# Six modulation chunks of the next layer: one per scan instead of all six ahead of the scans

## The chip, the cores and the metric

The kernel runs on one core of one Trainium2 chip. The metric is device time in microseconds (us) of one execution of the whole program, which computes both layers. The names of the engines here are: PE is TensorE (matrix products), DVE is VectorE, ACT is ScalarE, POOL is GpSimd, SP is SyncE, which in this kernel issues the loads of weights. PEld is the loading of the stationary operand, which goes beside PE.

## The reference, cut to what matters

One step of a diffusion backbone for 128 context and 256 latent tokens, two layers (`l` is 0, 1), model width 1024. Everything is float32.

```python
def trunk_layer(x, cvec, P, l, ctx=None, rope=None):
    mod = jnp.dot(jax.nn.silu(cvec), P['mod_w'][l]) + P['mod_b'][l]        # 1024 x 6144
    sh1, sc1, gt1, sh2, sc2, gt2 = jnp.split(mod[:, None, :], 6, axis=-1)
    h = rms_norm(x, P['norm1_g'][l]) * (1 + sc1) + sh1
    z = jnp.dot(h, P['w_in'][l])
    q, k, v, su, sv, rkv, xw, xa, xg, gates = split_cols(z, IN_SIZES)
    ...                                                # attention, gated MLP in chunks
    for d in range(2):                                 # RWKV-7, forwards and backwards
        s_fin, o_d = wkv_scan(s_init[d], r_h, heads(w_d), k_d, v_h, kk, heads(a_d), reverse=(d == 1))
    ...                                                # merge by gates, w_out
    x = x + gt1 * jnp.dot(merged, P['w_out'][l])
    h2 = rms_norm(x, P['norm2_g'][l]) * (1 + sc2) + sh2
    x = x + gt2 * moe(h2, P, l)                        # 64 experts, top 6, and a shared one

def wkv_scan(s0, r, w, k, v, kk, a, reverse):
    def step(s, inp):
        r_t, w_t, k_t, v_t, kk_t, a_t = inp
        sa = jnp.einsum('bhij,bhj->bhi', s, -kk_t)
        s = s * w_t[:, :, None, :] + sa[..., None] * (kk_t * a_t)[:, :, None, :] + v_t[..., None] * k_t[:, :, None, :]
        return s, jnp.einsum('bhij,bhj->bhi', s, r_t)
```

## The kernel before, in words

A loop runs twice, once per layer. Every engine has its program written out in order, and engines wait for each other on named semaphores; nothing is reordered by a scheduler. A layer goes through these stages: input projection (10 weight chunks), attention, gated MLP, six scans, merge, output projection, router and experts.

**Modulation.** The 6144 columns of `mod` are made in 16 chunks of 384 columns. A chunk is 1.5 MB of weights in one of two slots of SBUF (`slot0`, `slot1`). ACT copies the result to `mod_row` (`mod_rows`, line 635), and PE turns it to columns with three products with `sel` (`mod_turn`, six matmuls in the profile). Chunks 6 to 15 belong to this layer and are made during attention (10 calls, `c` from 0 to 9). Chunks 0 to 5 of the **next** layer (`c` from 10 to 15; MOD_B is 10 and MOD_A is 6) are made in one block on PE, lines 1647 to 1651, just ahead of the scans. They are gathered in PSUM bank 5 and DVE copies them to `next_mod` at once (line 1156).

**Slots.** Chunk n lies in slot n % 2. SP loads the next chunk of a slot when `slot_taken` of that slot has been raised. In the kernel before, a modulation chunk raises it with the first product of its turn, that is after ACT's copy.

**The scans.** `SCANS` lists six pairs of direction and chunk of 128 tokens, run in this order (scan 0 to 5). A scan of 128 steps is done by blocks: products of keys and queries within blocks (`block_grams`), then a triangular inverse by six levels. For each level PE does `level_y` for two groups, ACT copies the result to `YS` (line 765), PE does `level_x`, and DVE subtracts it (`invert`, line 1134); POOL prepares the block matrices `BL` (line 543). Between these, PE does `pair_grams` 0 to 3, which DVE masks (`mask_grams`, lines 1116 and 1118), and work of the scan before (`solve`, `results`) and for the scan after (`decay_or_rate`). In the last scan PE also does `bonus_and_gate` 0 to 3, and DVE the eight products of line 1191.

**What the first scan needs.** `block_grams(0)` waits for `queries_ready`, raised at line 1067 on DVE, the end of the chain of lines 1148 (a reciprocal of 128x1540 elements), 1149, 1058, 1062, 1066 and 1067. Lines 1071 to 1081 come behind it and raise `keys_ready`.

**PSUM.** During the scans banks 0, 6 belong to `level_y`, 1, 2 to `level_x`, 3, 4 to the grams and results, 5 and 7 to `decay_or_rate` (decays in 5, rates in 7), to `residue`, and in the last scan to `bonus_and_gate`.

## Time and profile before

| | us |
|---|---|
| median of 3 runs | 2624.59 (2624.20 to 2632.05) |
| the profiled execution's own time | 2626.4 |
| its span, first to last instruction | 2624.4 |
| PE busy in the span | 2262.4 (86%) |
| DVE busy | 1145.7 (44%) |
| ACT busy | 718.0 (27%) |
| mean granted clock of TensorE | 0.925 of 2.4 GHz |

Busy time of PE is from modelled ends of pipelined matmuls, so a PE that is busy is not a PE at its peak. The times of rows are counted from the start of the span. In a timeline row the columns are start, duration, engine, line, operation, output and inputs, shapes and count; the bracket at the end is the idle time of that engine before the row, and what ended it.

### The profile page before, as it was taken

What the parts mean: (1) busy time and instruction counts of PE and PEld (TensorE: products, weight loads), DVE (VectorE), ACT (ScalarE), POOL (GpSimd) and SP (SyncE); (2) the same over time, 40 slices, a digit from 0 to 9 for tenths busy, and PEclk for the clock granted to TensorE, in tenths of its full rate; (3) what the DMA queues carried; (4) which work ended last, traced back from release to release, by engine and by line L of the source; (5) the groups of instructions that cost most, each with busy time, mean ns of one, the idle gap of its engine ahead of it and who ended that gap; (6) DMA issues with size and microseconds to landing.
All of it is one profiled execution on the core that took longest, in us unless ns stands there. A gap on an engine that the chain in (4) does not pass through costs nothing.

```text
span 2624.4 us, 49132 instructions
## 1 busy us (share of the span) xinstructions
PE 2262.4 (86%) x20274; PEld 1704.3 (65%) x20274; DVE 1145.7 (44%) x1911; ACT 718.0 (27%) x1274; POOL 351.7 (13%) x389
## 2 busy tenths in 40 slices
PE   5999577888998878999679985888889978999996
PEld 4995367776887744555479753777668876555554
DVE  2357536554433612222264673555553345222224
ACT  3224334322212311222132233443222232221221
POOL 0000022210000132322100000221100002222320
PEclk8998789998999899999889895999989988999998
DMA  7325310000233298989543343000013253899896
GB/s 292 121 101 191 120 75 7 2 2 25 96 135 134 118 360 334 342 338 361 226 188 118 125 169 132 15 6 2 2 49 121 97 216 122 302 351 346 329 342 262
DMA packets 69267, 437.84 MB, mean 167 GB/s; under 512 B 23856, under 2 KB 26800, under 8 KB 37424
## 3 DMA queue, kind: packets, MB, share of 16 engines
q1 hardware_dynamic: 37504, 381.88, 37.7%
q0 software_dynamic: 28800, 37.83, 4.4%
q10 hardware_dynamic: 2736, 14.94, 1.4%
q8 instruction: 163, 2.67, 0.4%
q14 instruction: 64, 0.52, 0.1%
HBM read 545.96 MB, written 57.93 MB: 230 GB/s over the span
## 4 chain that ended last, share of the span: by engine, by line
PE 64%; DMA 14%; DVE 14%; issue 4%; ACT 3%; POOL 1%; SPq 0%; ACTq 0%; DVEq 0%; POOLq 0%
PE ps L1446 44%; DMA y_rows<-arena,mat 10%; PE ps L2023 8%; PE ps L2046 5%; DMA slot<-weights 2%; PE ps L2010 2%; DMA h_room<-weights 1%; DVE arena L1134 1%; DVE W_lo L440 1%; PE ps L2064 1%; DVE arena L1220 1%; DVE arena L1118 1%; PE ps L2033 1%; DVE arena L1039 1%; PE ps L1942 1%
## 5 line engine op out<-in xcount | busy, mean ns | idle before, releaser
L1446 PE MATMUL ps<-arena 64*64 64x64 f32 (+5 forms) x8704 | 465.2, 244 | 95.0 <-POOL arena L543 22.1
L1446 PEld LDWEIGHTS ps<-arena 64*64 64x64 f32 (+3 forms) x8704 | 397.2, 148 | 155.6 <-issue 47.6
L1446 PE MATMUL ps<-H_hi,W_lo 128*128 128x384 f32 x768 | 267.4, 348 | 30.7 <-DVE H_lo L934 25.2
L2023 PE MATMUL ps<-arena 128*64 128x256 f32 x1408 | 268.6, 390 | 20.8 <-ACT arena L846 17.0
L1446 PE MATMUL ps<-H_hi,W_hi 128*128 128x384 f32 x768 | 262.6, 342 | 0.0
L1446 PE MATMUL ps<-H_lo,W_hi 128*128 128x384 f32 x768 | 262.5, 342 | 0.0
L434 ACT ACTIVATE W_hi<-slot 128x3072 fp32r<-128x3072 f32 x44 | 121.9, 2770 | 381.1 <-DMA slot<-weights 171.8
L2023 PEld LDWEIGHTS ps<-arena 128*64 128x64 f32 x1408 | 155.6, 140 | 99.3 <-ACT arena L846 19.3
L543 POOL TENSOR_TENSOR arena<-arena,con 128x256 f32<-128x256 f32 x144 | 109.2, 758 | 814.9 <-ACT arena L750 563.7
L440 DVE TENSOR_TENSOR W_lo<-slot,W_hi 128x3072 fp32r<-128x3072 f32 x44 | 147.8, 3358 | 144.2 <-ACT W_hi L434 143.8
L2023 PE MATMUL ps<-h_room,arena 128*64 128x256 f32 x768 | 176.1, 382 | 0.0
L1351 DVE COPY arena<-ps 128x512 f32<-128x512 f32 x100 | 69.1, 691 | 242.1 <-DMA y_rows<-arena,mat 172.7
L1446 PEld LDWEIGHTS ps<-H_hi,W_lo 128*128 128x128 f32 x768 | 146.3, 191 | 34.3 <-DVE W_lo L440 32.5
L1134 DVE TENSOR_TENSOR arena<-arena,ps 128x512 f32<-128x512 f32 x120 | 82.4, 687 | 186.6 <-PE ps L1446 184.2
L1358 DVE SCALAR_TENSOR_TENSOR mat<-mat,ps 128x128 f32<-128x128 f32 x100 | 34.7, 347 | 264.9 <-ACT mat L876 264.9
L1446 PEld LDWEIGHTS ps<-H_lo,W_hi 128*128 128x128 f32 x768 | 146.1, 190 | 1.9
L2046 PE MATMUL ps<-arena,mat 128*64 128x512 f32 x352 | 139.0, 605 | 8.6 <-DVE mat L1367 8.4
L1446 PEld LDWEIGHTS ps<-H_hi,W_hi 128*128 128x128 f32 x768 | 146.1, 190 | 0.0
L583 POOL DMA_INDIRECT y_rows<-arena,mat x100 | 100.6, 1006 | 302.6 <-DVE arena L1351 287.4
L564 POOL DMA_INDIRECT arena<-h_rows,mat x100 | 101.9, 1019 | 234.5 <-PE ps L2010 215.1
L852 ACT ACTIVATE arena<-ps 128x512 f32<-128x512 f32 x100 | 59.7, 597 | 257.7 <-DMA y_rows<-arena,mat 181.9
L1446 PE MATMUL ps<-branches,slot 128*128 128x384 f32 x384 | 126.4, 486 | 0.0
(285 smaller groups left out, 3711.1 us busy)
## 6 DMA issues: line engine op xcount, KB each, us to landing
slot<-weights SPq DMA_DIRECT2D x130, 1536.0 KB, 6.8
arena<-weights SPq DMA_DIRECT2D x92, 1536.0 KB, 10.5
h_room<-weights ACTq DMA_DIRECT2D x48, 1536.0 KB
branches<-weights ACTq DMA_DIRECT2D x24, 1536.0 KB
arena<-y_rows SPq DMA_DIRECT2D x8, 1536.0 KB, 18.0
slot<-y_rows SPq DMA_DIRECT2D x4, 1536.0 KB, 8.2
mat<-params SPq DMA_DIRECT2D x3, 1664.0 KB, 12.0
h_room<-weights SPq DMA_DIRECT2D x2, 1536.0 KB, 27.1
```

Source lines behind the costliest of these rows:

```text
L434: do(eng.activation(W_hi[m % 2][:, :], w, ACT.Copy), hi_ready)
L440: do(eng.tensor_tensor(W_lo[m % 2][:, :], slot[n % SLOTS][:, :], W_hi[m % 2][:, :].bitcast(F32), ALU.subtract), slot_taken[n % SLOTS], n / ...
L543: do(eng.tensor_tensor(BL[:, g, :].rearrange("p (u t) -> p u t", u=4), GB[:, 4 * g:4 * g + 4, :], con[:, None, m:m + HALF_P].to_broadcast( ...
L564: eng.indirect_dma_start(ROWS_IN[i % X_RING], None, h2_dram, bass.IndirectOffsetOnAxis(from_row[:, c:c + 1], 0), bounds_check=T - 1, oob_i ...
L583: eng.indirect_dma_start(y_dram, bass.IndirectOffsetOnAxis(to_row[:, c:c + 1], 0), YO[:, i % 2, :], None, bounds_check=T * TOP_K - 1, oob_ ...
L852: eng.activation(YO[:, i % 2, 0:512], ps[:, 6, :], ACT.Copy).then_inc(yo_act, 1)
L1134: do(eng.tensor_tensor(XG4, XG4, ps[:, 1 + g, :].rearrange("p (u x t) -> p u x t", u=4, x=2), ALU.subtract), inv_ready)
L1351: eng.tensor_copy(YO[:, i % 2, 512:1024], ps[:, 7, :]).then_inc(yo_dve, 1)
L1446: mm = eng.matmul(*args, **kw)
L2010: mm = eng.transpose(ps[:, k // 4, (k % 4) * P:(k % 4 + 1) * P], ROWS_IN[i % X_RING][:, k * P:(k + 1) * P], ident)
L2023: mm = eng.matmul(ps[o, 2 + i % 2, 0:256], XT[:, i % 2, k, o], w[h][0][:, k * 256:(k + 1) * 256], start=(k == 0), stop=(k == KD - 1))
L2046: mm = eng.matmul(ps[o, 6 + q, :], hidT[:, i % 2, o], w[h][0][:, 2 * D + q * 512:2 * D + (q + 1) * 512], start=True, stop=True)
```

## The change

`mod_chunk` now raises `slot_taken` with its last product, and ACT's `mod_rows` waits for that count; the semaphore `mod_row_filled` is gone. The block ahead of the scans is gone from PE and ACT. In scan n PE makes chunk 10 + n in bank 5 after `pair_grams(n, 0)`, ahead of `level_x(n, 2, 0)`; ACT copies it after the two `YS` copies of level 2; PE turns it into columns 448 to 453 of bank 7 after `pair_grams(n, 2)`, ahead of `level_x(n, 3, 0)`; DVE copies six columns to `next_mod` after `mask_grams(n, 2)`. `residue(n)` waits for that copy, and so does `bonus_and_gate(0)` in the last scan. The wait of `decay_or_rate(1, 0)` for the copy of line 1156 is gone.

```diff
@@ ACT
                 def mod_rows(c, bank):
-                    eng.wait_ge(mod_row_filled, c + 1)
+                    eng.wait_ge(slot_taken[(C_MODB + c) % SLOTS], (C_MODB + c) // SLOTS + 1)
                     do(eng.activation(mod_row[:, c % 2, :], ps[:, bank, 0:3 * P], ACT.Copy), mod_row_ready)
...
-                for c in range(MOD_B, MOD_B + MOD_A):
-                    mod_rows(c, 6 + c % 2)
...
+                        if lv == 2:
+                            mod_rows(MOD_B + n, 5)
@@ DVE
-                eng.wait_ge(modb_filled, MOD_B + 1)
-                do(eng.tensor_copy(next_mod[:, :, :], ps[:, 5, 0:6 * MOD_A].rearrange("p (m g) -> p m g", g=2)), modb_ready)
+                def keep_next(n):
+
+                    eng.wait_ge(modb_filled, MOD_B + n + 1)
+                    do(eng.tensor_copy(next_mod[:, 3 * n:3 * n + 3, :], ps[:, 7, NEXT_AT:NEXT_AT + 6].rearrange("p (m g) -> p m g", g=2)),
+                       modb_ready)
...
                     mask_grams(n, 2)
+                    keep_next(n)
                     invert(n, 3, 0)
@@ PE
                     if k1 == KD:
-                        mm.then_inc(mod_row_filled, 1)
+                        mm.then_inc(slot_taken[(C_MODB + c) % SLOTS], 1)
...
-                        if m == 0:
-                            mm.then_inc(slot_taken[(C_MODB + c) % SLOTS], 1)
...
                 eng.wait_ge(kk_root, QT)
-                for c in range(MOD_B, MOD_B + MOD_A):
-                    mod_chunk(c, 6 + c % 2)
-                    if c > MOD_B:
-                        mod_turn(c - 1, 5, 6 * (c - 1 - MOD_B))
-                mod_turn(MOD_B + MOD_A - 1, 5, 6 * (MOD_A - 1)).then_inc(modb_filled, 1)
                 eng.wait_ge(turned_ready, NT + 1)
...
                     eng.wait_ge(gram_ready, 8 * n + 8)
+                    eng.wait_ge(modb_ready, MOD_B + n + 1)
...
                     if j:
                         eng.wait_ge(bonus_done, 2 * j)
                         eng.wait_ge(outgate_ready, j)
+                    else:
+                        eng.wait_ge(modb_ready, MOD_B + MOD_A)
...
                         if n:
                             eng.wait_ge(r_ready, 2 * n)
-                        else:
-                            eng.wait_ge(modb_ready, MOD_B + 1)
                         decay_or_rate(n + 1, 0)
...
                     pair_grams(n, 0)
+                    if more:
+                        eng.wait_ge(decay_ready, 4 * n + 8)
+                    else:
+                        eng.wait_ge(r_ready, 2 * n)
+                    mod_chunk(MOD_B + n, 5)
                     level_x(n, 2, 0)
...
                     pair_grams(n, 2)
+                    if more:
+                        eng.wait_ge(rate_ready, 4 * n + 8)
+                    mod_turn(MOD_B + n, 7, NEXT_AT).then_inc(modb_filled, 1)
                     if not more:
                         bonus_and_gate(0)
                     level_x(n, 3, 0)
```

The first place is PE just ahead of the scans and in scan 0. In the kernel before, `slot,csil` is a modulation chunk, `con,mod_row` its turn, and the first `arena 64x64 x24` is `block_grams(0)`:

```order
L1446 MATMUL ps<-arena,mat 128x128 x8
L1644 MATMUL ps<-con,arena 128x128 x12
L1446 MATMUL ps<-slot,csil 32x384 x16
L1446 MATMUL ps<-con,mod_row 128x2 x3
L1446 MATMUL ps<-slot,csil 32x384 x8
L1446 MATMUL ps<-con,mod_row 128x2 x3
L1446 MATMUL ps<-slot,csil 32x384 x8
L1446 MATMUL ps<-con,mod_row 128x2 x3
L1446 MATMUL ps<-slot,csil 32x384 x8
L1446 MATMUL ps<-con,mod_row 128x2 x3
L1446 MATMUL ps<-slot,csil 32x384 x8
L1446 MATMUL ps<-con,mod_row 128x2 x6
```

In the changed kernel the same place reads as follows, down to `level_x` of level 2 (`64x64 x16` behind the chunk):

```order
L1452 MATMUL ps<-arena,mat 128x128 x8
L1648 MATMUL ps<-con,arena 128x128 x12
L1452 MATMUL ps<-arena 64x64 x24
L1452 MATMUL ps<-arena,mat 128x128 x4
L1452 MATMUL ps<-con,arena 64x64 x16
L1452 MATMUL ps<-arena,mat 128x128 x4
L1452 MATMUL ps<-arena 64x64 x64
L1452 MATMUL ps<-arena 128x256 x2
L1452 MATMUL ps<-arena 128x128 x2
L1452 MATMUL ps<-slot,csil 32x384 x8
L1452 MATMUL ps<-arena 64x64 x16
```

The six chunks and turns ahead of `block_grams(0)` are gone, and one chunk stands between `pair_grams(0, 0)` (`128x256 x2`, `128x128 x2`) and `level_x(0, 2, 0)`.

The second place is PE in the last scan, from `pair_grams(5, 2)` to `pair_grams(5, 3)`. Here `arena,mat 128x384` and `arena,con 128x384` are `bonus_and_gate(0)`. Before:

```order
L1446 MATMUL ps<-arena 128x256 x2
L1446 MATMUL ps<-arena 128x128 x2
L1446 MATMUL ps<-arena,mat 128x384
L1446 MATMUL ps<-arena,con 128x384
L1446 MATMUL ps<-arena 64x64 x16
L1446 MATMUL ps<-arena 128x256 x2
```

and in the changed kernel:

```order
L1452 MATMUL ps<-arena 128x256 x2
L1452 MATMUL ps<-arena 128x128 x2
L1452 MATMUL ps<-con,mod_row 128x2 x3
L1452 MATMUL ps<-arena,mat 128x384
L1452 MATMUL ps<-arena,con 128x384
L1452 MATMUL ps<-arena 64x64 x16
```

The turn stands ahead of `bonus_and_gate(0)`, which now also waits for DVE's copy of it.

The third place is DVE in the same scan of the changed kernel, where line 1196 is the last of eight products for the bonus, 1117 and 1119 are `mask_grams(5, 2)`, 1159 the new copy and 1135 `invert(5, 3, 0)`:

```order
L1196 SCALAR_TENSOR_TENSOR arena<-arena,vec 128x128
L1196 SCALAR_TENSOR_TENSOR arena<-arena,vec 128x256
L1117 TENSOR_TENSOR arena<-ps,con 128x2x128
L1119 TENSOR_TENSOR arena<-ps,con 128x2x256
L1159 COPY next_mod<-ps 128x6
L1135 TENSOR_TENSOR arena<-arena,ps 128x512
```

The copy is the one row that is new there; PE's `bonus_and_gate(0)` is behind it.

## Rows read from the trace of the kernel before

**Rows 1.** The page, busy time, share of the span and instructions of each engine.

```profile
PE 2262.4 (86%) x20274; PEld 1704.3 (65%) x20274; DVE 1145.7 (44%) x1911; ACT 718.0 (27%) x1274; POOL 351.7 (13%) x389
```

**Rows 2.** Stretches: from:to and length, busy per engine, granted clock, DMA share, GB/s.

```profile
291.00:343.00 52.00, 20.86 (x133) 10.16 (x133) 18.89 (x15) 12.11 (x24) 0.00 (x0) 0.57 0.34 121
...
345.00:640.00 295.00, 244.21 (x4647) 212.58 (x4645) 152.12 (x255) 100.73 (x211) 59.98 (x78) 0.92 0.03 12
...
1634.90:1674.30 39.40, 32.93 (x682) 29.99 (x682) 20.49 (x36) 17.26 (x37) 8.74 (x12) 0.87 0.18 76
```

**Rows 3.** Timeline of PE, first layer, from the block to `block_grams(0)`.

```profile
290.93 2.79 PE L1446 MATMUL ps<-slot,csil 128*32 128x384 f32 x32
302.07 1.44 PE L1446 MATMUL ps<-con,mod_row 128*128 128x2 f32 x6 [8.36 <-ACT mod_row L635]
309.18 2.79 PE L1446 MATMUL ps<-slot,csil 128*32 128x384 f32 x16 [5.67 <-DMA slot<-weights]
...
338.78 2.79 PE L1446 MATMUL ps<-slot,csil 128*32 128x384 f32 x16 [5.59 <-DMA slot<-weights]
...
343.00 1.16 PE L1446 MATMUL ps<-arena 64*64 64x64 f32 x48
```

**Rows 4.** Timeline of DVE in the same stretch.

```profile
293.98 9.78 DVE L1148 RECIPROCAL arena<-arena 128x1540 f32<-128x1540 f32 x1
...
307.76 0.69 DVE L1067 TENSOR_TENSOR arena<-arena 128x512 f32<-128x512 f32 x1
```

**Rows 5.** Timelines of DVE and PE at the same place of the second layer.

```profile
1598.27 0.69 DVE L1067 TENSOR_TENSOR arena<-arena 128x512 f32<-128x512 f32 x1
...
1634.93 1.99 PE L1446 MATMUL ps<-arena 64*64 64x64 f32 x48
```

**Rows 6.** Timeline of PE, a chunk and a turn at full clock, during attention.

```profile
190.61 1.50 PE L1446 MATMUL ps<-slot,csil 128*32 128x384 f32 x16 [0.64 <-ACT arena L652]
192.04 0.33 PE L1552 MATMUL ps<-con,arena 128*128 128x128 f32 x1
...
194.36 0.73 PE L1446 MATMUL ps<-con,mod_row 128*128 128x2 f32 x6
```

**Rows 7.** Timeline of PE and DVE in scan 2, levels 2 and 3.

```profile
438.42 2.00 PE L1446 MATMUL ps<-arena 64*128 64x256 f32 x40 [0.54 <-DVE mat L1108]
...
441.17 0.69 DVE L1134 TENSOR_TENSOR arena<-arena,ps 128x512 f32<-128x512 f32 x1
...
444.79 2.61 PE L1446 MATMUL ps<-arena 64*64 64x64 f32 x56 [1.14 <-POOL arena L543]
...
447.63 0.69 DVE L1134 TENSOR_TENSOR arena<-arena,ps 128x512 f32<-128x512 f32 x1
```

**Rows 8.** Timelines of PE and DVE in scan 3, level 2.

```profile
485.28 5.80 PE L1446 MATMUL ps<-arena 64*128 64x256 f32 x96 [1.30 <-DVE mat L1108]
...
488.80 0.69 DVE L1134 TENSOR_TENSOR arena<-arena,ps 128x512 f32<-128x512 f32 x1 [0.61 <-PE ps L1446]
```

**Rows 9.** Timeline of PE and DVE in scan 5, level 3.

```profile
587.49 0.91 PE L1446 MATMUL ps<-arena,mat 128*128 128x384 f32 x2
...
588.98 1.15 PE L1446 MATMUL ps<-arena 64*64 64x64 f32 x32
...
590.63 0.69 DVE L1118 TENSOR_TENSOR arena<-ps,con 128x512 f32<-128x512 f32 x1
591.35 0.69 DVE L1134 TENSOR_TENSOR arena<-arena,ps 128x512 f32<-128x512 f32 x1
```

**Rows 10.** Line 1156: count, duration in ns (least/median/most), first and last start.

```profile
L1156 DVE COPY next_mod<-ps x2: 194/194/195, 343.2 to 1635.1; 128x36 f32<-128x36 f32 x2
```

**Rows 11.** Timeline of PE, the same point of scan 0 in either layer.

```profile
353.97 2.61 PE L1446 MATMUL ps<-arena 64*64 64x64 f32 x56 [0.96 <-POOL arena L543]
...
1648.61 2.61 PE L1446 MATMUL ps<-arena 64*64 64x64 f32 x56 [0.96 <-POOL arena L543]
```

**Rows 12.** DMA issues from 280 to 400 us: count, size, median us to landing.

```profile
slot<-weights SPq DMA_DIRECT2D x6, 1536.0 KB, 6.2
```

4 lines of the change are left out of this document (2 added, 2 removed).

## The prediction

> **What bounds the kernel now.** I read the page first: PE is busy for 86% of the span [rows 1], so on the average the kernel is bound by PE. An average hides stages with other limits, so I next took the stretches. From 291 to 343 us, the block of six chunks, PE is busy for 20.86 of 52 us, at a granted clock of 0.57, with DMA at a third [rows 2]. The reader should see there a stage bound by something else than PE. The timeline of PE shows what: the first two chunks run at once, PE then waits 8.36 us for ACT's copy, and every further chunk waits about 5.6 us for its load: I count four such waits in this layer, of which the first and the last are shown [rows 3]. A load takes 6.2 us from issue to landing [rows 12], and the period of 338.78 - 309.18 = 29.6 us for three chunks is 9.9 us a chunk: load, products (2.79 us), turn. The scans begin only when all six are done, at 343.00 [rows 3], and at 1634.93 in the second layer [rows 5].
>
> The scans themselves are another matter. From 345 to 640 us PE is busy for 244 of 295 us [rows 2], in a chain from PE over ACT or POOL to DVE and back, in which each engine has short waits for the next.
>
> **What is removed.** The block goes. What then releases `block_grams(0)`? Its own wait is for line 1067 of DVE. The reciprocal of 9.78 us from 293.98 holds DVE, and line 1067 ends at 307.76 + 0.69 = 308.45 [rows 4]; in the second layer it ends at 1598.27 + 0.69 = 1598.96 [rows 5]. So the block's cover is used in part: 291 to 308.5 was needed by DVE anyway, and PE will stand idle there. With 0.05 us for the release, `block_grams(0)` moves from 343.00 to 308.50 and from 1634.93 to 1599.01. That is 34.5 + 35.9 = **70.4 us gained**. The keys (lines 1071 to 1081, three operations behind line 1067) are asked for first by `pair_grams(0, 0)`, in the group of rows 11, which begins 10.97 us after `block_grams(0)`; so they don't hold it. The old copy of line 1156 (0.19 us [rows 10]) hung on the block and is in that difference.
>
> **What is added to PE.** Each scan gets a chunk and a turn. At full clock a chunk holds PE for 192.04 - 190.61 = 1.43 us and a turn for 0.73 us, which I take as 0.75 [rows 6]; at half clock they are 2.79 and 1.44 us [rows 3]. If nothing hid them, six of each would be 13.1 us a layer at full clock and 25.4 at half clock. What hides some is slack at the place.
>
> Scan 2, level 2: `pair_grams` and `level_x` run together from 438.42 to 440.42, with no gap between them, so ACT's copy was no limit and the chunk delays `level_x` by all of 1.43, to 441.85. DVE took its result at 441.17, since it was masking until then. With 0.1 us for the release it takes it at 441.95: 0.8 us late. Level 3: the group with `level_x` ends at 444.79 + 2.61 = 447.40 and DVE takes it at 447.63. It ends now at 447.40 + 0.8 + 0.75 = 448.95, so DVE goes at 449.05, 1.4 us late [rows 7]. DVE's new copy (0.19 us [rows 10], for fewer columns) stands where DVE waits for PE, so it costs nothing here; where that wait is gone it costs its 0.2 us. Scan 3: DVE waits 0.61 us for PE at level 2 [rows 8], so there is no slack and all of 1.43 is paid, and with 0.5 at level 3 the scan loses 1.95 us. I take the middle of these two, 1.7 us, for scans 0 to 4: 8.5 us a layer.
>
> In scan 3 the 96 matmuls take 5.80 us [rows 8], where in scan 2 the first 40 alone took 2.00 [rows 7]: part of that stretch ran at half clock. A chunk that falls in it would be 2.79 us. But if the stretch at half clock keeps its length, the work behind the chunk escapes it, so the added time is near the full-clock price. I take this; the other end goes to the range.
>
> **The last scan.** Here a wait is added. `bonus_and_gate(0)` waits for DVE's copy, which stands behind `mask_grams(5, 2)`, and behind PE's waiting instruction are `level_x(5, 3, 0)` and `pair_grams(5, 3)`, for which DVE waits. Before, `bonus_and_gate(0)` began at 587.49, `level_x` ended at 588.98 + 1.15 = 590.13, and the mask ended at 590.63 + 0.69 = 591.32, with `invert` at 591.35 [rows 9]. From 587.49 to 590.13 is 2.64 us of PE work. The chunk shifts DVE by 1.4 at level 2, so the mask ends at 592.7 and the copy at 592.95. PE then goes on: 593.0 + 2.64 = 595.65, and `invert` starts at 595.7, 4.35 us late. The turn itself is hidden under the mask. So the last scan costs 4.35 us, 2.9 of it by the new wait.
>
> **The clock at the start.** In the first layer scan 0 began at 343.00 and came to the group of rows 11 after 10.97 us; in the second it took from 1634.93 to 1648.61, 13.68 us [rows 3, 5, 11], and its stretch had a clock of 0.87 [rows 2]. So a cold start costs 2.7 us. After the change PE does nothing from about 291 to 308.5 us. I take it that both layers start cold, so the first pays 2.7 us more.
>
> The Trainium skill has a rule that speaks against this change here: "TensorE: Matmul & The Clock Gate", section "HAM oscillation — how this bites in real kernels", says that PE waits between bursts drop the clock to half, so that each burst starts cold. By that rule the block's chunks run cold, as the trace agrees (2.79 us against 1.50), and the idle PE ahead of the scans makes the first scan begin cold; without the rule the first layer would keep its warm start, and the sum would be 2.7 us lower.
>
> **Edits at nothing.** The slots are also released earlier during attention, ahead of ACT's copy; but in the timeline of PE I see waits for a load only in the block [rows 3], none in attention, so nothing there gets earlier. In the scans a load of 6.2 us [rows 12] has a whole scan of some 40 us before its chunk is asked for. The merge's first two chunks are loaded during scans 4 and 5 and not scan 0; the later one is released at level 2 of scan 5, more than 20 us before the merge. If that cover failed it would cost at most a load, 6.2 us a layer. ACT's copy of `mod_row` stands behind the `YS` copies, and ACT waits for PE there.
>
> **The sum.** Added per layer: 8.5 + 4.35 = 12.85, for two 25.7; cold start 2.7; together 28.4. Gained 70.4. Net -42.0 us. Against the profiled execution's own 2626.4 us that is 2584.4; its own time is 1.8 us over the median, so I forecast **2583 us** as the median.
>
> **The rivals.**
> 1. The scans hide nearly all of it, because waits not seen as slack (POOL's level matrices, the tables that ACT loads) take it up. For it: each group of level_x is followed by a wait in rows 7. Against: DVE takes `level_x`'s result within 0.75 us of its end in both. With only the last scan's wait left, 2 x 2.9 + 2.7 = 8.5 added: 2626.4 - 1.8 - 70.4 + 8.5 = 2563 us. Between this and the forecast lies a half-hidden case at about 2572.
> 2. Chunks and turns meet half clock each time and pay it: 12 x (2.79 + 1.44 + 0.19) = 53.0, and 2 x 2.9 and 2.7: 61.5 us added, 2615.7 us. For it: scans 3 and following have cold pieces just at level 2 [rows 8]. Against: the clock over the scans is 0.92 [rows 2]. With cold chunks in half of the scans and the full price for the others, I get (53.0 + 12 x 2.2) / 2 + 8.5 = 48 added, 2602 us.
> 3. The change doesn't do what it says: something else holds scan 0. The other thing that could is ACT's copy of the values, but PE's first turn in rows 3 shows ACT through with them by 302. If half of the 70.4 us were lost to such a wait: 2624.6 - 35.2 + 28.4 = 2618 us.
> 4. Slower than before: the clock. The scans live near the edge of the clock's fall (0.92 mean, 0.57 in the block [rows 2]). If the long idle stretch and the new work let the clock stay at 1.2 GHz through the scans, every cold us costs by rows 11: about 10.6 us were cold in the second layer's start for 2.7 us lost, 0.25 each. All of 2 x 270 us of scans would cost 135 us and give 2718 us. It decides from 42.0 / 0.25 = 168 us of more cold scan. Against: PE is denser with the change, and the clock recovered within 11 us in the second layer.
>
> **How the numbers follow.** The forecast with its own spread of 2576 to 2590: 0.6. Rival 1 with the half-hidden case: 0.17. Rival 2: 0.16, mostly at its middle case. Rival 3: 0.04. Rival 4: 0.03. The range runs from 2567 (between the half-hidden and the hidden case) to 2598 (nearly rival 2's middle case), and leaves out some 0.1 on each side. A measurement of this kernel tells about 0.3%, 7.9 us, from no change. Faster by more: all but rival 4, the far end of rival 2 and a part of rival 3: 0.95. Within it: 0.02. Slower: 0.03.
>
> **What would show it.** `block_grams(0)` starting within 0.3 us of the end of DVE's line 1067 chain, some 34 us earlier. No PE wait for a load between attention and merge. One chunk of about 1.5 us in each scan, scans 0 to 4 longer by 1.4 to 2.0 us and scan 5 by 4 to 5, with a PE wait of about 4 us ahead of `bonus_and_gate(0)` that DVE's copy ends. The first scan of both layers at half clock for some 10 us. Wrong would be: a new wait of PE on loads in a scan, scans longer by more than 3 us each, or `block_grams(0)` held by another wait than DVE's.

## The result, and the profile after

The changed kernel takes 2602.35 us (median of 4 runs, 2594.38 to 2606.01) against 2627.14 us for the kernel before on the same chip (2624.2 to 2632.05): a ratio of 0.9901, with an interval of 0.9877 to 0.9925. It is faster by 1%: 26 us by the ratio, 24.8 by the two medians, where the prediction said 42.0. The median lies 4.4 us above the range of 2567 to 2598.

The profiled execution took 2594.38 us. The page begins:

```profile
span 2592.4 us, 49178 instructions
...
PE 2265.2 (87%) x20274; PEld 1714.4 (66%) x20274; DVE 1146.5 (44%) x1921; ACT 717.9 (28%) x1274; POOL 351.1 (14%) x389
```

PE did the same 20274 products in 2.8 us more busy time [rows 1], and the span is 32.0 us shorter than the 2624.4 us of before. Work was moved, not removed.

The first place is the start of the scans. This is the timeline of PE in the kernel after, from the first layer (the last two rows are from scan 4 and from the second layer):

```profile
289.70 1.53 PE L1648 MATMUL ps<-con,arena 128*128 128x128 f32 x12
308.83 1.98 PE L1452 MATMUL ps<-arena 64*64 64x64 f32 x48 [17.61 <-DVE arena L1068]
...
322.87 1.53 PE L1452 MATMUL ps<-arena 64*64 64x64 f32 x24 [0.61 <-issue]
324.33 1.50 PE L1452 MATMUL ps<-slot,csil 128*32 128x384 f32 x16
325.76 3.55 PE L1452 MATMUL ps<-arena 64*64 64x64 f32 x88
...
512.42 2.75 PE L1452 MATMUL ps<-slot,csil 128*32 128x384 f32 x16
...
1582.39 1.98 PE L1452 MATMUL ps<-arena 64*64 64x64 f32 x48 [17.61 <-DVE arena L1068]
```

The block is gone: behind the turned values (line 1648) PE waits 17.61 us for DVE and then starts `block_grams(0)`, which took 1.16 us in the first layer before [rows 3] and takes 1.98 now, since the clock is at its lower level. The chunk of scan 0 runs at full clock (1.50 us), that of scan 4 at half clock (2.75).

The rest is read from stretches. I cut the scans at the first turned key of each (line 1690 before, 1689 after), so that a row is one scan, the first of them from `block_grams(0)`. Stretches of the kernel before (from:to and length, busy per engine, granted clock, DMA share, GB/s), with both layers as a whole, scans 0 and 1 in either layer, and scans 2 to 5 in the first:

```profile
343.00:595.00 252.00, 210.34 (x4334) 187.43 (x4333) 141.07 (x236) 91.84 (x196) 58.64 (x76) 0.95 0.04 16
1634.93:1887.03 252.10, 212.09 (x4333) 189.24 (x4332) 141.02 (x236) 91.83 (x196) 58.70 (x76) 0.95 0.04 15
...
343.00:367.27 24.27, 19.35 (x450) 17.04 (x449) 14.66 (x27) 13.41 (x28) 8.00 (x11) 1.00 0.34 132
1634.93:1661.90 26.97, 23.50 (x450) 21.27 (x449) 14.66 (x27) 13.40 (x28) 8.01 (x11) 0.80 0.26 110
...
367.27:409.79 42.52, 35.54 (x764) 32.66 (x761) 24.72 (x41) 17.22 (x37) 10.01 (x13) 0.96 0.01 3
1661.90:1703.21 41.31, 34.20 (x764) 31.21 (x761) 24.72 (x41) 17.22 (x37) 10.08 (x13) 1.00 0.01 3
...
409.79:451.28 41.49, 34.16 (x764) 31.20 (x761) 24.61 (x42) 17.50 (x38) 10.46 (x14) 1.00 0.01 3
451.28:498.91 47.63, 40.54 (x796) 35.91 (x793) 25.30 (x43) 17.50 (x38) 9.85 (x13) 0.93 0.02 8
498.91:546.73 47.82, 40.53 (x795) 35.84 (x793) 25.55 (x43) 17.50 (x38) 10.12 (x13) 0.93 0.01 2
546.73:595.00 48.27, 40.22 (x784) 34.78 (x781) 26.22 (x45) 8.71 (x21) 10.20 (x13) 0.93 0.01 2
```

and the same of the kernel after, the whole of both layers and the six scans of the first:

```profile
308.83:581.95 273.12, 233.84 (x4465) 203.21 (x4465) 143.66 (x244) 94.77 (x202) 58.79 (x76) 0.91 0.11 38
1582.39:1855.03 272.64, 233.64 (x4465) 203.32 (x4465) 143.39 (x244) 94.77 (x202) 58.24 (x76) 0.91 0.11 38
...
308.83:337.58 28.75, 26.24 (x470) 23.22 (x471) 16.54 (x30) 13.90 (x29) 7.96 (x11) 0.78 0.16 57
337.58:382.08 44.50, 37.76 (x785) 33.60 (x782) 24.88 (x42) 17.99 (x38) 9.97 (x13) 0.96 0.11 38
382.08:426.24 44.16, 37.73 (x786) 33.60 (x783) 24.78 (x43) 17.99 (x38) 10.45 (x14) 0.96 0.12 44
426.24:475.98 49.74, 42.93 (x817) 37.19 (x815) 25.55 (x44) 17.99 (x38) 9.74 (x13) 0.93 0.10 35
475.98:528.72 52.74, 45.79 (x818) 38.94 (x815) 25.47 (x44) 17.99 (x38) 10.56 (x14) 0.87 0.09 32
528.72:581.95 53.23, 43.39 (x806) 36.67 (x803) 26.44 (x46) 8.91 (x21) 10.11 (x13) 0.90 0.08 32
```

Three things are to be seen. From the turned values to `block_grams(0)` it was 53.53 and 54.97 us, and is 19.13 in both layers: 70.2 us gained. The scans grew from 504.1 to 545.8 us: 41.7 us lost. The rest of the span is 3.5 us shorter. That makes the 32.0. And the clock: where it stayed alike, a scan grew by 1.98 us (scan 1, both at 0.96) and by 2.11 (scan 3, both at 0.93); where it fell, by 2.67 (scan 2, from 1.00 to 0.96) and by 4.92 (scan 4, from 0.93 to 0.87). In the second layer scan 2 kept the full clock and grew by 1.25 us, from 41.49 to 42.74.

The clock has a price that these rows give. At a mean clock c a stretch of length t held 2 x (1 - c) x t us at half clock (1.2 GHz instead of 2.4). Scan 1 of before has the same work in both layers: 42.52 us with 3.4 us at half clock, 41.31 with none. So a half-clock us cost 1.21 / 3.4 = 0.35 us. (Scan 0 gives (26.97 - 24.27) / 10.6 = 0.25, the figure of the prediction.) Scans 1 and 2 of the kernel after, each with 3.4 us more or less of half clock in one layer than in the other, give 0.29 (45.49 against 44.50 us) and 0.42 (44.16 against 42.74). I use 0.35 below, as an estimate that can be off by a fifth either way, and by more in scan 0. The lengths of half clock in the tables below are taken from the clock record of the traces, and agree with that formula.

The last scan is the other place that the prediction named. Timelines of PE and DVE in the kernel after:

```profile
570.18 0.83 PE L1452 MATMUL ps<-con,mod_row 128*128 128x2 f32 x6
574.32 1.62 PE L1452 MATMUL ps<-arena,mat 128*128 128x384 f32 x2 [3.31 <-DVE next_mod L1159]
575.73 1.49 PE L1452 MATMUL ps<-arena,con 128*128 128x384 f32 x2
577.15 3.64 PE L1452 MATMUL ps<-arena 64*64 64x64 f32 x88
...
573.29 0.69 DVE L1119 TENSOR_TENSOR arena<-ps,con 128x512 f32<-128x512 f32 x1
574.01 0.16 DVE L1159 COPY next_mod<-ps 128x6 f32<-128x6 f32 x1
578.51 0.69 DVE L1135 TENSOR_TENSOR arena<-arena,ps 128x512 f32<-128x512 f32 x1 [4.33 <-PE ps L1452]
```

PE has the turn done at 571.01 and waits 3.31 us for the copy that stands behind DVE's mask; then DVE waits 4.33 us for PE's `level_x`. Before, line 1134 followed the mask at once [rows 9].

### The profile page after: what moved, and what is told of

Same layout as the page of the kernel before. It is cut to its first block, busy times and chain, and to the rows that moved or that the text cites. A ratio compares the mean times of both kernels' runs of the same rounds, so it can differ in the third digit from the quotient of the medians.

```text
span 2592.4 us, 49178 instructions
## 1 busy us (share of the span) xinstructions
PE 2265.2 (87%) x20274; PEld 1714.4 (66%) x20274; DVE 1146.5 (44%) x1921; ACT 717.9 (28%) x1274; POOL 351.1 (14%) x389
## 4 chain that ended last, share of the span: by engine, by line
PE 66%; DVE 14%; DMA 12%; issue 4%; ACT 2%; POOL 1%; SPq 0%; ACTq 0%; DVEq 0%; POOLq 0%
PE ps L1452 47%; DMA y_rows<-arena,mat 10%; PE ps L2031 9%; PE ps L2054 5%; PE ps L2018 2%; DVE W_lo L441 1%; DMA h_room<-weights 1%; DMA arena<-y_rows 1%; DVE arena L1135 1%; DVE arena L1226 1%; DVE arena L1149 1%; DVE arena L1383 1%; PE ps L2041 1%; ACT W_hi L435 1%; PE ps L1950 1%
## 5 line engine op out<-in xcount | busy, mean ns | idle before, releaser
L1452 PE MATMUL ps<-arena 64*64 64x64 f32 (+5 forms) x8704 | 477.1, 249 | 121.1 <-DVE arena L1068 35.2
L1452 PEld LDWEIGHTS ps<-arena 64*64 64x64 f32 (+3 forms) x8704 | 408.7, 153 | 188.3 <-issue 95.9
## 6 DMA issues: line engine op xcount, KB each, us to landing
arena<-weights SPq DMA_DIRECT2D x92, 1536.0 KB, 10.5
mat<-params SPq DMA_DIRECT2D x3, 1664.0 KB, 12.3
```

Source lines behind the costliest of these rows:

```text
L1452: mm = eng.matmul(*args, **kw)
```

## The experiments

Each was timed against the kernel before on its own chip, whose medians there were 2626.09 to 2628.26 us. Where products are said to be unread, nothing uses their result. Half-clock figures are of one profiled execution each.

### The change in two parts

**e4_slots_alone**, on the kernel before: the block stays where it was, and only the slots are given back by the chunk's last product.

```diff
-                    eng.wait_ge(mod_row_filled, c + 1)
+                    eng.wait_ge(slot_taken[(C_MODB + c) % SLOTS], (C_MODB + c) // SLOTS + 1)
...
-                        mm.then_inc(mod_row_filled, 1)
+                        mm.then_inc(slot_taken[(C_MODB + c) % SLOTS], 1)
...
-                        if m == 0:
-                            mm.then_inc(slot_taken[(C_MODB + c) % SLOTS], 1)
```

> The kernel before with one part of the change alone: the slots are given back by a chunk's last product, and ACT waits for that count; the block of six chunks stays ahead of the scans. Each of the block's four loads starts earlier by ACT's copy and the first matmul of the turn, about 0.8 us, and the first two by the 8.4 us that PE waited for ACT there. Theory A: the block is bound by loads that wait for slots, so it shortens by some 8 + 2 x 0.8 us a layer, about 10 us of its 52, 20 us in all: ratio 0.992. Rival: the loads are bound by the DMA queue itself (6.2 us each, one after another) so only the first start counts, 6 us a layer: ratio 0.995. Second rival: the attention stage gains too, which would show as an earlier start of the block.

Measured: 2579.03 us, ratio 0.9839 (0.981 to 0.9867). This half of the change alone gains 47 us by the medians and 42 by the ratio, more than the whole: its interval lies clear below that of the kernel after (0.9877 to 0.9925). It is also more than twice the 20 us that were expected. Its PE timeline in the block:

```profile
289.98 2.79 PE L1446 MATMUL ps<-slot,csil 128*32 128x384 f32 x32
301.12 1.44 PE L1446 MATMUL ps<-con,mod_row 128*128 128x2 f32 x6 [8.36 <-ACT mod_row L635]
302.49 2.79 PE L1446 MATMUL ps<-slot,csil 128*32 128x384 f32 x16
305.21 1.44 PE L1446 MATMUL ps<-con,mod_row 128*128 128x2 f32 x6
306.58 2.79 PE L1446 MATMUL ps<-slot,csil 128*32 128x384 f32 x16
309.30 0.93 PE L1446 MATMUL ps<-con,mod_row 128*128 128x2 f32 x6
313.45 2.79 PE L1446 MATMUL ps<-slot,csil 128*32 128x384 f32 x16 [3.22 <-DMA slot<-weights]
...
320.04 1.16 PE L1446 MATMUL ps<-arena 64*64 64x64 f32 x48
```

Before, each slot was held through ACT's copy and until the turn, so that the wait of 8.36 us and then each load stood one behind the other [rows 3]. Now the loads of the third and fourth chunk run while PE waits for ACT, and one wait of 3.22 us is left of four of 5.6 to 6.0. `block_grams(0)` starts 31.52 us behind the turned values, where it was 53.53 before and is 19.13 in the kernel after. In the two layers that is 44.4 us gained in the block; the scans are 5.6 us shorter, with less time at half clock (table below). So the second half, the move into the scans, brings 12.4 and 13.4 us in the block (31.52 and 32.55 against 19.13) and costs 47.3 in the scans (498.5 to 545.8).

**e10_four_ahead_two_at_waits**, on the kernel after: four chunks stand ahead of the scans again, and two in scans 0 and 1, made behind the turned keys where PE waits for ACT, and turned ahead of `pair_grams` of the next scan.

```diff
+                for c in range(MOD_B, MOD_B + 4):
+                    mod_chunk(c, 6 + c % 2)
+                    if c > MOD_B:
+                        mod_turn(c - 1, 5, 6 * (c - 1 - MOD_B))
+                mod_turn(MOD_B + 3, 5, 18).then_inc(modb_filled, 1)
...
+                    if 0 < n < 3:
+                        eng.wait_ge(rate_ready, 4 * n + 8)
+                        mod_turn(MOD_B + n + 3, 7, NEXT_AT).then_inc(modb_filled, 1)
                     pair_grams(n, 0)
...
                     turn_keys(n)
+                    if n < 2:
+                        eng.wait_ge(decay_ready, 4 * n + 8)
+                        mod_chunk(MOD_B + n + 4, 5)
```

> As the run before it, but four chunks ahead of the scans (the third and fourth are loaded while PE waits for ACT's first copy) and two in scans 0 and 1. Where the block of six with slots given back early ended at 320 us, four end at 310, 1.5 us after DVE's chain. Theory A: 2579 (the block of six) less 2 x 10 us, and 1 us of growth: about 2561 us, ratio 0.975. Theory C (an idle PE ahead of the scans spoils their clock): here PE is busy up to the scans, so the half-clock time in the scans is 10 to 20 us a layer as in the block of six, and this run is faster than the one with two ahead.

Measured: 2566.40 us, ratio 0.9768 (0.975 to 0.9787), the best version of all, 60 us faster than before and faster than both kernels. Its stretches:

```profile
312.99:563.61 250.62, 213.19 (x4378) 188.67 (x4377) 141.29 (x238) 92.71 (x198) 58.47 (x76) 0.96 0.07 23
1569.07:1821.31 252.24, 214.77 (x4378) 189.62 (x4377) 141.37 (x238) 92.72 (x198) 58.61 (x76) 0.95 0.06 22
```

`block_grams(0)` starts 22.43 us behind the turned values, so four chunks need only 3.3 us beyond DVE's chain of 19.13, and the scans are as short as before the change.

**e7_two_ahead_four_at_waits** is the same with two chunks ahead and four at the waits of scans 0 to 3.

> Another placement of the same work, with slots given back by the last product: chunks 0 and 1 of the next layer, which have landed, are made in PE's idle stretch ahead of the scans; chunks 2 to 5 are made in scans 0 to 3 behind the turned keys, where PE waits 1.8 us for ACT, and turned in scans 1 to 4 ahead of the first pair of grams, where it waits 1.3 us for DVE. Theory A (a scan pays for a chunk only what the place has no slack for): the scans begin at 308.5 us as in the changed kernel, each of four scans grows by less than 0.5 us, the last one not at all: 2627 - 70 + 3 + 3 = 2563 us, ratio 0.976. Theory C: the clock takes back some 14 us in the scans: 2577 us, ratio 0.981.

Measured: 2570.45 us, ratio 0.9784 (0.9754 to 0.9814). Here `block_grams(0)` starts as early as in the kernel after (19.13 us behind the turned values), but the scans take 257.3 and 253.7 us. The intervals of e7 and e10 overlap.

**e11_act_copies_first** is e4 with ACT's first two copies of a chunk ahead of its exponentials.

```diff
                 rates(0)
+                mod_rows(MOD_B, 6)
+                mod_rows(MOD_B + 1, 7)
                 exponentials(0)
```

> The block of six chunks ahead of the scans, with slots given back by the last product, and ACT's copies of the first two chunks moved ahead of its exponentials, so that PE's first turn does not wait 8.4 us for ACT and the third and fourth chunk are made as they land. Loads of about 4.5 us then follow one another from 292 us, the last lands near 309, and the scans begin near 312 us instead of 320, with nothing added to them. Theory: 2579 - 2 x 8 = 2563 us, ratio 0.976, equal to or under the run with four chunks ahead. Rival: the third and fourth chunk still wait for ACT, whose later copies stand behind its work for the scans, and the scans begin at 317 or later: 2573 us.

Measured: 2576.01 us, ratio 0.9816 (0.9794 to 0.9839): as e4. PE's wait of 8.36 us for ACT is gone, and in its place stand waits of 4.40, 2.56 and 0.66 us for loads; `block_grams(0)` starts 29.38 and 30.92 us behind the turned values, where e4 had 31.52 and 32.55. That is the expectation's rival (2573 us) and not its theory (2563): with six chunks ahead the block is bound by its loads, which fits that two fewer of them gained in e10.

### What the cold start costs

**e3_pe_kept_busy** and **e8_idle_filled**, on the kernel after: 20 and 27 unread products of 384 columns in PE's wait for DVE.

```diff
                 eng.wait_ge(kk_root, QT)
+                for i in range(27):
+                    matmul(ps[:, 7, 0:T], heads, CV[:, 8 + i % 4, 0:T], start=True, stop=True)
                 eng.wait_ge(turned_ready, NT + 1)
```

> The changed kernel with 20 products of 384 columns, whose result nobody reads, put where PE is idle for 17.6 us ahead of the first scan of each layer. Theory A: the clock is at 2.4 GHz when the scans begin, scan 0 loses its cold start (28.7 us from the first block grams to the turned keys becomes about 26), and the time falls by 2 x 2.7 = 5.4 us against the changed kernel, ratio 0.988. Theory C (the idle stretch sets how the clock behaves in the later scans too): the half-clock time in scans 1 to 5 falls from about 37 us a layer towards the 24 of the kernel before as well, and the time falls by 12 us or more. Rival: nothing changes, since the chain of the scans and not PE's clock sets scan 0; then the time stays at 2602.

> The changed kernel with 27 products of 384 columns (result unread) ahead of the first scan, which at 0.65 us each last until PE's wait for DVE ends, where 20 of them ended 4.7 us early and the clock had fallen again by the first block grams. Theory C (the idle stretch starts the scans cold): the clock is 2.4 GHz at the first block grams, and from there to the turned keys of scan 0 takes about 26 us instead of 28.7 in both layers; half-clock time in that scan falls from 12 us to near 0. The time falls by some 5 us against the changed kernel. If the idle stretch also shifts what comes later, half-clock time in scans 1 to 5 falls from 37 to about 24 us a layer and the time by 12 or more. Rival: the clock falls at the start of the scans by itself; nothing moves.

Measured: e3 2605.47 us, ratio 0.9934 (0.9908 to 0.996); its products ended 4.70 us before DVE was done, the clock had fallen again, and scan 0 still took 28.74 us, so it told nothing. e8 closed that gap to 0.19 us: 2595.24 us, ratio 0.9878 (0.9854 to 0.9902), and its stretches are

```profile
310.92:336.62 25.70, 21.41 (x471) 18.21 (x471) 16.35 (x30) 13.90 (x29) 7.99 (x11) 1.00 0.17 64
310.92:580.45 269.53, 228.96 (x4465) 197.73 (x4465) 143.74 (x244) 94.79 (x202) 57.67 (x76) 0.93 0.11 38
1580.71:1853.56 272.85, 232.15 (x4465) 200.42 (x4465) 143.65 (x244) 94.77 (x202) 57.87 (x76) 0.92 0.11 38
```

Scan 0 fell from 28.75 to 25.70 us at a clock of 1.00: the cold start costs 3.05 us a layer, and the chunk and turn cost scan 0 25.70 - 24.27 = 1.43. But scans 1 to 5 stayed long and held 37.5 and 44.4 us at half clock. The idle PE ahead isn't the reason for those.

**e9_little_block**, on e4: one of eight products of a chunk, and one of three of a turn, stay in the block.

```diff
-                    mod_chunk(c, 6 + c % 2)
+                    w1 = landed(eng, C_MODB + c).rearrange("p (k n) -> p k n", k=KD)
+                    matmul(ps[0:32, 6 + c % 2, 0:3 * P], csil[:, 0:32], w1[:, 0, :], start=True, stop=True).then_inc(slot_taken[(C_MODB + c) % SLOTS], 1)
```

> The kernel before with slots given back by the last product, the six chunks in their block ahead of the scans, but with one of eight products and one of three turns of each (the modulation is not computed). The scans hold no load, no added product, no added wait, and begin after a block in which PE is nearly idle. Theory B (loads or waits inside the scans cost time or clock): half-clock time in the scans is 17 to 27 us a layer and their length that of the kernel before, about 252 us from first block grams to the last turned keys. Theory C (the clock of the scans depends on how idle PE was ahead of them and not on what was put into them): half-clock time is near 50 us a layer and the length near 265, as in the run with little work in the scans. The block itself should take about 25 us (two landed chunks, four loads of some 4.5 us), so the scans begin near 313 us.

Measured: 2604.45 us, ratio 0.9921 (0.9902 to 0.994). That time can't be used, as a late stage whose routing hangs on the values ran some 25 us longer. The scans can: 252.09 us at a clock of 0.95 in the first layer, as in the kernel before, and 253.7 in the second. They began cold (26.91 and 26.95 us for scan 0), and held 17 and 20 us at half clock behind it, no more than the kernel before (24 and 17). This too says that an idle PE ahead costs the start alone.

### What makes the scans slow

**e1_little_work**, on the kernel after: the same cut as e9's, but in the scans.

> The changed kernel, but in the scans only one of a chunk's eight products is done and one of its three turns (so the next layer's modulation is not computed); the loads, the copies of ACT and DVE and every wait stay. Theory A (the 21 us that the scans of a layer grew by come from PE's added work and from the clock that this work meets): what is left of the growth is the wait of the last scan, 2.9 us a layer, a cold start and some 0.3 us a scan, about 12 us in all, so 2627 - 70 + 12 = 2569 us, ratio 0.978. Theory B (the loads of 1.5 MB that now run during the scans slow the engines): the growth stays near 20 us a layer, the time near 2600 us, ratio 0.990. Theory C (the clock is lower in the scans whatever PE does there, because they start after an idle stretch): half-clock time in the scans stays at about 50 us a layer as in the changed kernel's profile and the time is about 2580 us.

Measured: 2578.57 us, ratio 0.9823 (0.9793 to 0.9853), 24 us faster than the kernel after by the medians. The profiled execution (2583.18 us, the slowest of four) shows scans of 271.5 and 265.7 us with 51 and 34 us at half clock behind scan 0. The scans are 8.6 us shorter in all than in the kernel after, though they hold 10 us more at half clock, so fewer products do cost less. But the time at half clock is not proportional to them. The time is that of theory C; its cause, the idle stretch ahead, is ruled out by e8 and e9.

**e13_no_copies**, on the kernel after: loads and PE's work stay, ACT's and DVE's copies and the waits for them go.

```diff
-                        if lv == 2:
-                            mod_rows(MOD_B + n, 5)
...
-                    keep_next(n)
...
-                    eng.wait_ge(modb_ready, MOD_B + n + 1)
...
-                    else:
-                        eng.wait_ge(modb_ready, MOD_B + MOD_A)
```

> The changed kernel with the loads and PE's chunks and turns in the scans, but without ACT's and DVE's copies of them and without the waits for these copies (so the next layer's modulation is not computed; the turns use constants). Theory A: the last scan's interval falls by 2.9 us a layer, and the rest stays, 2597 us. If the copies and waits are what brings the clock down, half-clock time in the scans falls from 49 us a layer to under 30 and the time to about 2585 us; if loads or PE's work do, it stays at 40 or more.

Measured: 2590.55 us, ratio 0.9865 (0.9844 to 0.9886). The last scan falls from 53.23 to 50.3 us, 2.9 us a layer; scans 0 to 4 take 221.5 us in either layer, where the kernel after had 219.9 and 219.4, and 41 us at half clock behind scan 0 is no less than its 37.5. So copies and their waits don't bring the clock down.

**e2_turn_early_last**, on the kernel after: in the last scan the turn stands after `pair_grams(5, 1)`, and DVE's copy after `mask_grams(5, 1)`.

```diff
                     pair_grams(n, 1)
+                    if not more:
+                        mod_turn(MOD_B + n, 7, NEXT_AT).then_inc(modb_filled, 1)
                     level_x(n, 2, 1)
```

> The changed kernel, but in the last scan alone the turn stands after the second pair of grams instead of the third, and DVE's copy after the second mask, so that the copy is long done when the bonus products ask for it. Theory A: the 2.9 us of new wait a layer go, the last scan (turned keys of scan 4 to those of scan 5) falls from 53.2 to 50.3 us, the time by 5.8 us against the changed kernel: about 2597 us, ratio 0.988. Rival: the last scan grew by the clock and the chunk and not by this wait; then the interval stays within 1 us of 53.2 and the time at 2602.

Measured: 2597.64 us, ratio 0.9892 (0.9855 to 0.9928). PE's wait of 3.31 us is gone, and the last scan takes 51.09 and 49.64 us instead of 53.23. The medians don't tell that from the kernel after.

**e12_work_alone_in_scans**, **e14_chunks_alone** and **e15_turns_alone**, on e4: its block stays, and unread products of the shapes of a chunk and a turn, or one of the two, stand at the places of the change, with the waits on `decay_ready` or `r_ready` and on `rate_ready` ahead of them.

```diff
                     pair_grams(n, 0)
+                    if more:
+                        eng.wait_ge(decay_ready, 4 * n + 8)
+                    else:
+                        eng.wait_ge(r_ready, 2 * n)
+                    for k in range(KD):
+                        r = slice(32 * (k % 4), 32 * (k % 4 + 1))
+                        matmul(ps[r, 5, 0:3 * P], csil[:, 2 * k:2 * k + 32], con[:, 0:3 * P], start=(k < 4), stop=(k >= 4))
                     level_x(n, 2, 0)
...
                     pair_grams(n, 2)
+                    if more:
+                        eng.wait_ge(rate_ready, 4 * n + 8)
+                    for m in range(3):
+                        matmul(ps[:, 7, 448 + 2 * m:450 + 2 * m], con[:, m * P:(m + 1) * P], c_("sel", 2), start=True, stop=True)
```

> The block of six with slots given back early, and besides it, in each scan at the two places of the change, products of the same shapes as a chunk and a turn, on constants, whose result nobody reads: PE's work alone is added, with no load, no copy of ACT or DVE and no wait for one. Against the block of six (2579 us): Theory A (PE's work costs what the places have no slack for): scans 0 to 4 grow by about 1.7 us and scan 5 by 1.5 to 2, some 21 us in all, 2600 us. Theory D (PE's work at these places also makes the clock fall more often): half-clock time in the scans goes from 14 to 20 us a layer to over 35, and the growth is 35 us or more, 2614 us. Theory B (loads, copies or waits do that): half-clock time stays under 25 us.

> The block of six with slots given back early, with only the unread products of a chunk's shape added at level 2 of each scan. Theory A: 12 x 1.2 = 14 us of direct price, 2593 us. Theory D (the chunk's products bring the clock down): half-clock time in the scans of 40 us or more a layer, against 14 to 20 without them, and some 8 us more, 2602 us; if the turns are what does it, half-clock time stays under 25 us a layer.

> The same with only the unread products of a turn's shape at level 3 of each scan. Theory A: 12 x 0.5 = 6 us of direct price, 2585 us, half-clock time under 25 us a layer. If the turns are what brings the clock down (a full stationary load for two columns each), half-clock time of 40 us or more a layer and 2595 us.

**e16_work_at_waits** has the same products, in scans 0 to 4, at e10's places: the chunk's behind the turned keys, the turn's ahead of `pair_grams(n, 0)`.

> The same work as in the run with both added (chunk and turn shapes, unread), in scans 0 to 4, but the chunk behind the turned keys, where PE waits 1.8 us for ACT, and the turn ahead of the first pair of grams, where it waits 1.3 us for DVE from scan 1 on. Theory A: nearly all of it is hidden, under 0.5 us a scan, 2583 us. If it is the work and not its place that brings the clock down, half-clock time is 40 us or more a layer, as with both at the places of the change, and the time is about 2592 us; if it is the place, half-clock time stays under 25.

**e6_chunk_twice**, on the kernel after: each chunk of the scans is made twice (12 times 1.43 = 17.2 us of PE more).

```diff
+                    mod_part(matmul, landed(eng, C_MODB + MOD_B + n).rearrange("p (k n) -> p k n", k=KD), 5, 0, KD)
                     mod_chunk(MOD_B + n, 5)
```

> The changed kernel with the eight products of a chunk done twice in each scan, which adds 12 x 1.43 = 17.2 us of PE work at full clock. Theory A (a chunk is paid in full once the slack of its place is used up): the time rises by 17 us against the changed kernel, 2619 us, ratio 0.997. Rival (each chunk meets half clock): 12 x 2.79 = 33 us, 2635 us. Rival (the places still have slack, the growth was clock alone): under 8 us.

Measured: e12 2615.55 us, ratio 0.9947 (0.9926 to 0.9967); e14 2606.16, 0.9918 (0.9884 to 0.9952); e15 2592.59, 0.9866 (0.983 to 0.9902); e16 2589.71, 0.9848 (0.9814 to 0.9881); e6 2600.56, 0.9911 (0.988 to 0.9941), as the kernel after. Against their expectations: e12 came out as theory D, in time and in clock. e14 had the time of its theory D, but 27 and 40 us at half clock in the scans of a layer where it wanted 40 or more in each. e15 lies 8 us above theory A with 24 and 34 us, and e16 lies 7 us above its own, with 35 and 31. e6 has the number of its last rival, under 8 us more than the kernel after, but not its reason: where the half clock is as long as in the kernel after, the second chunk costs 1.3 us in scan 0 (30.04 against 28.75), 1.1 in scan 1 (46.56 against 45.49) and 1.3 in scan 2 (44.03 against 42.74). The stretches of e4 are

```profile
320.04:568.15 248.11, 206.61 (x4333) 183.53 (x4332) 141.36 (x236) 91.83 (x196) 58.59 (x76) 0.97 0.04 13
1583.73:1834.16 250.43, 209.33 (x4334) 186.54 (x4333) 141.00 (x236) 91.84 (x196) 58.63 (x76) 0.96 0.03 11
```

and those of e12

```profile
327.24:595.87 268.63, 231.19 (x4466) 200.61 (x4465) 141.18 (x236) 91.83 (x196) 58.98 (x76) 0.92 0.03 10
1610.73:1882.70 271.97, 234.52 (x4465) 203.41 (x4465) 140.90 (x236) 91.84 (x196) 59.56 (x76) 0.91 0.03 11
```

e12 has no load, no copy and no new wait for DVE in its scans (DMA share 0.03, DVE and ACT busy as in e4), and yet they are nearly as long as in the kernel after. Products on PE, with the waits ahead of them, do it alone. And those waits hold nothing up: in the traces of the kernel after, e1, e6, e8 and e12 to e15, PE goes on to each of the added groups without a gap, as in the rows at 324.33 and 570.18 us above. All kernels side by side, the two layers apart, in us:

| kernel | added in the scans of a layer | scans | half clock in scan 0 | half clock in scans 1 to 5 |
|---|---|---|---|---|
| before | nothing | 252.0, 252.1 | 0, 10.6 | 23.9 + 17.1 = 41 |
| e4 | nothing | 248.1, 250.4 | 0, 0 | 13.7 + 20.5 = 34 |
| e11 | nothing | 252.0, 252.0 | 0, 10.9 | 23.9 + 17.1 = 41 |
| e9 | nothing | 252.1, 253.7 | 10.4, 10.5 | 17.1 + 20.5 = 38 |
| e10 | 2 chunks, 2 turns, at waits | 250.6, 252.2 | 0, 0 | 20.5 + 23.9 = 44 |
| e16 | 5 chunks, 5 turns, at waits | 255.7, 254.1 | 10.8, 10.2 | 23.9 + 20.5 = 44 |
| e7 | 4 chunks, 4 turns, at waits | 257.3, 253.7 | 12.5, 12.2 | 30.7 + 20.5 = 51 |
| e15 | 6 turns | 254.0, 256.4 | 3.4, 9.9 | 20.5 + 23.9 = 44 |
| e14 | 6 chunks | 261.2, 264.4 | 0, 13.0 | 27.3 + 27.3 = 55 |
| e6 | 12 chunks, 6 turns | 275.2, 278.4 | 12.5, 12.3 | 23.9 + 30.7 = 55 |
| after | 6 chunks, 6 turns | 273.1, 272.6 | 12.5, 12.2 | 37.5 + 37.5 = 75 |
| e2 | 6 chunks, 6 turns | 272.6, 269.1 | 12.3, 12.2 | 41.0 + 34.1 = 75 |
| e12 | 6 chunks, 6 turns | 268.6, 272.0 | 10.2, 10.2 | 34.1 + 41.0 = 75 |
| e8 | 6 chunks, 6 turns | 269.5, 272.9 | 0, 0 | 37.5 + 44.4 = 82 |
| e13 | 6 chunks, 6 turns | 271.8, 271.8 | 12.4, 12.4 | 41.0 + 41.0 = 82 |
| e3 | 6 chunks, 6 turns | 276.2, 276.2 | 12.3, 12.3 | 44.4 + 44.4 = 89 |
| e1 | 6 and 6, one product each | 271.5, 265.7 | 12.2, 12.3 | 51.2 + 34.1 = 85 |

Each kernel has one trace, but kernels whose scans are alike repeat each other. In the eight layers with nothing added, half clock in scans 1 to 5 is 13.7 to 23.9 us; in the twelve with all six chunks and turns at the change's places it is 34.1 to 44.4. These two groups don't overlap, so the increase is no chance of one execution.

With 0.35 us for each half-clock us (taken for scan 0 too), e14's 27.1 us of longer scans against e4 are 11.7 of clock and 15.4 of direct price, 1.3 a scan; e15's 11.8 are 8.2 and 3.6, 0.3 a scan; and e16's 11.2 are 10.9 and 0.3, next to nothing. e16 shows it without the clock as well: its scan 1 takes 41.39 us at full clock, against 41.31 before. So at the waits the products are free as such. They also bring little or no half clock behind scan 0 there: the six layers of e7, e10 and e16 have 20.5 to 30.7 us, 23 on the average, against 19 with nothing added. Only at the change's own places does it go to 34 and more. e16 adds nothing in the last scan, but the difference is there without it: in scans 1 to 4 it holds 17.1 and 10.2 us, where e12 holds 27.3 and 34.1. What e16 has over e4 at half clock lies mostly in scan 0 (10.8 and 10.2 us), where kernels with nothing added have 0 in some layers and 10.4 to 10.9 in others.

## Why the prediction was wrong

**The block: right.** 70.4 us were predicted and 70.2 measured. `block_grams(0)` starts 0.14 us behind the end of DVE's line 1068 (308.00 + 0.69), and PE waits on no load between attention and the merge.

**Scans 0 to 4: right as a direct price.** 1.7 us each was predicted; at an unchanged clock scan 0 shows 1.43 (e8), scan 1 1.98, scan 2 1.25 and scan 3 2.11, 1.7 on the average, and e14 and e15 give 1.3 + 0.3.

**The last scan: right.** 4.35 us were predicted, and 53.23 - 48.27 = 4.96 measured in the first layer, with 3.4 us more at half clock among them (1.2). The wait was 3.31 us, where 2.9 was its share; e13 takes it away and gets 2.9 back.

**The cold start: right.** 2.7 us for the first layer were predicted and e8 shows 3.05; the second layer was cold before too. The rule of the Trainium skill ("TensorE: Matmul & The Clock Gate", "HAM oscillation — how this bites in real kernels") holds for this start.

**The clock inside the scans: wrong.** This is the step that failed: "if the stretch at half clock keeps its length, the work behind the chunk escapes it, so the added time is near the full-clock price. I take this". The stretches did not keep their length. Behind scan 0 the half clock went from 41 to 75 us in the two layers; 34 more at 0.35 are 12 us (10 to 14 with the other prices from the rows). With that, the 41.7 us that the scans grew by are 3.05 for the start, 12 for the clock and the rest, 26.6, direct, where 2.7, 0 and 25.7 were predicted. The prediction's argument against rival 4, that PE is denser with the change, points the wrong way too: PE was denser, and the clock lower.

**Rival 2: its number, not its mechanism.** Its middle case, cold chunks in half of the scans, gave 2602 us, which is what was measured. That is luck. In the trace of the kernel after ten of the twelve chunks ran at full clock (1.50 us), and only the two of scan 4 at half (2.75 and 2.67). The chunks hardly met half clock; with them there was more of it elsewhere in the scans.

The profiled execution is thus 10.0 us short of the predicted gain: 13.3 in the scans and 0.2 in the block, less the 3.5 gained elsewhere. Its own time, 2594.38 us, lies within the range. The median is another 9.4 us farther from the forecast: the profiled execution was the fastest of its four, 8.0 us under their median, while the forecast took 1.8 us off for before's. The other three had a clock of 0.921 or 0.922 over the whole span, against 0.925. From 0.925 to 0.922 that is 2 x 0.003 x 2595 = 16 us more at half clock, or 5 to 6 us by the same price. Only one execution has a trace, but the mean clock is on record for all. In 105 executions of the kernels here, each compared with others of its own kernel on its chip, a us more at half clock went with 0.32 us more of time (correlation 0.8, where 1 is a straight line). So the clock also makes much of the spread between executions, and the 3 to 4 us that are left of the 9.4 I can't place.

**An edit at nothing: wrong, though it did not move this sum.** The prediction set the earlier release of the slots at nothing, and looked for its effect in attention. It never asked what it does with the block in place. e4 is the answer: 42 to 47 us. The change itself could not show this, since it also removes the block; but whoever reads that the move gained 26 us misreads it. With the release made, the move loses: 23 us by the two medians, 16 by the two ratios, 17.4 between the two profiled executions.

**What stays open.** That the products at these two places lengthen the half clock is shown by e12 against e4; I have not settled what it is in them that does it. It isn't the loads or copies (e12, e13), not the idle PE ahead (e8, e9), and not a wait on `decay_ready` or `rate_ready`, since by the traces PE never stands there. It isn't in proportion to the products: one eighth of them (e1) left it high, and twice the chunks (e6) brought it down from 75 to 55 us. e6's 17.2 us more of PE work made the scans 7.9 us longer, and 20.5 us less at half clock give back 7.2, which nearly closes that account. Chunks alone (e14, 27.3 us in both layers) lie a little above the scans with nothing added, and turns alone (e15) among them; neither makes the 34 to 44 of both together. Between such neighbours, some 10 us apart, one trace each doesn't decide.

## What to carry to other kernels

Before work is moved out of a stage that waits for loads, look at when its buffers are given back: an edit of four lines there gained more than the whole change. Work belongs where the engine waits anyway, and only as much of it as the stage's own bound (here DVE's chain, 19.13 us) leaves uncovered is worth moving. Sum a chain on PE at its measured clock, but keep a term for the clock itself: in this chain with short gaps, added products went with nearly twice the half-clock time, though most of them ran at full clock themselves, and the same products at PE's waits with little or none.

## What the runs showed of the hardware

More work on PE went with less clock. In the scans before, PE was busy for 83% of the time (210.34 of 252.00 us) at a mean clock of 0.95; with 131 more matmuls among 4334, at 86% (233.84 of 273.12 us, a share that the slower clock itself raises), the clock was 0.91. It is no rule even here: e6, with 96 matmuls more than that, had 0.93 and 0.92. By the Trainium skill's rule one would look for gaps between bursts: "TensorE: Matmul & The Clock Gate", "A second HAM failure mode: psum-queue depth-cycling", says that frequent micro-idles between groups of products can make the clock oscillate. The scans have such gaps (eight of 0.24 to 1.73 us in scan 3 of the kernel before), but that rule alone doesn't say why the same products bring more of it at one place than at another, and these runs don't either.

In this chain a us at half clock cost 0.29 to 0.42 us, by single scans that differ in nothing else, and 0.32 over whole executions. A stretch in which PE alone set the pace would do half a us of work in it and so lose 0.5; the chain's waits for DVE, ACT and POOL take up a part, though I haven't measured which.
